# Attention rounds: scores three steps ahead, outputs of two blocks taken together a step later, denominators spread over three steps

## What is computed

```python
a = a_val * jax.nn.sigmoid(a_gate)
a = jax.nn.silu(layer_norm(causal_depthwise_conv(a, conv_w, conv_b), ln_g, ln_b))     # 31 taps, 512 channels
...
s = jnp.einsum('bqhd,bqkhd->bqhk', qb, k_sel) * (HEAD_DIM ** -0.5)                    # 8 heads of 64
p = jax.nn.softmax(jnp.where(valid[:, :, None, :], s, -jnp.inf), axis=-1)
o = jnp.einsum('bqhk,bqkhd->bqhd', p, v_sel)
...
return jnp.concatenate([a, o], axis=-1) @ w_out
```

## Time and profile before

| | us |
|---|---|
| median of three runs | 2775.15 |
| lowest and highest run | 2771.99, 2776.19 |
| span of the profiled execution | 2768.8 |
| of it, the stage `attention_and_conv` with its first loads | about 420 to 720 |
| loops 0 to 41 with their start, with taps | 434 to 595 |
| loops 42 to 71 and the end of the stage, no taps | 595 to 720.5 |

### The profile page before, as it was taken

How to read it: one execution, slowest core, us unless ns; L and a number is a source line. 1 busy time by engine, 2 the same in 40 slices (tenths; PEclk the granted TensorE clock), 3 DMA queues, 4 the chain that set the end, 5 groups by cost and what they waited for, 6 DMA issues and landing times. The chain is left out here.

```text
span 2768.8 us, 37693 instructions
## 1 busy us (share of the span) xinstructions
PE 2483.0 (90%) x12607; PEld 2105.9 (76%) x12607; DVE 2035.1 (74%) x2461; ACT 1707.5 (62%) x1832; POOL 643.2 (23%) x484
## 2 busy tenths in 40 slices
PE   8789987997895999999999589997969999999993
PEld 8779966876584888888888478986857888888882
DVE  4687775667657898888988644545468888888895
ACT  2367836655423778787777446555127777777773
POOL 0105616643001211211121212121001112222213
PEclk9899998997896999999999789999979999999996
DMA  5502233220535879998899411003347879999994
GB/s 169 124 1 93 75 95 91 83 56 6 153 107 202 330 252 365 367 375 293 293 367 361 166 66 38 32 30 110 106 161 260 320 262 371 367 366 370 374 364 145
DMA packets 115273, 565.16 MB, mean 204 GB/s; under 512 B 23520, under 2 KB 27872, under 8 KB 65904
## 3 DMA queue, kind: packets, MB, share of 16 engines
q1 hardware_dynamic: 89776, 512.15, 50.7%
q0 software_dynamic: 25408, 51.84, 6.9%
HBM read 574.22 MB, written 74.34 MB: 234 GB/s over the span
## 5 line engine op out<-in xcount | busy, mean ns | idle before, releaser
L1923 DVE TENSOR_TENSOR e0wlo<-e0raw,e0whi 128x2048 fp32r<-128x2048 f32 x214 | 486.9, 2290 | 68.6 <-ACT e0whi L1771 67.0
L1923 DVE TENSOR_TENSOR e1wlo<-e1raw,e1whi 128x2048 fp32r<-128x2048 f32 x208 | 472.9, 2289 | 66.0 <-ACT e1whi L1771 66.0
L1771 ACT ACTIVATE e0whi<-e0raw 128x2048 fp32r<-128x2048 f32 x214 | 410.0, 1916 | 103.2 <-PE e0u L90 42.1
L1771 ACT ACTIVATE e1whi<-e1raw 128x2048 fp32r<-128x2048 f32 x208 | 398.3, 1916 | 101.0 <-PE e1u L90 42.1
L88 PE MATMUL odd_ps<-h2T_hi,odd_w_hi 128*128 128x348 f32 x480 | 158.3, 330 | 6.2 <-DVE odd_w_lo L2388 6.2
L89 PE MATMUL odd_ps<-h2T_lo,odd_w_hi 128*128 128x348 f32 x480 | 155.6, 324 | 0.0
L90 PE MATMUL odd_ps<-h2T_hi,odd_w_lo 128*128 128x348 f32 x480 | 155.4, 324 | 0.0
L88 PE MATMUL m_y<-m_whi,m_xhi 128*128 128x512 f32 (+1 forms) x304 | 121.7, 400 | 22.1 <-DVE m_wlo L1503 21.6
L89 PE MATMUL m_y<-m_wlo,m_xhi 128*128 128x512 f32 (+1 forms) x304 | 119.7, 394 | 0.0
L90 PE MATMUL m_y<-m_whi,m_xlo 128*128 128x512 f32 (+1 forms) x304 | 119.7, 394 | 0.0
L88 PE MATMUL e0g<-e0whi,e0xh 128*128 128x512 f32 x284 | 115.6, 407 | 0.6 <-DVE e0xl L1928 0.6
(11 more groups left out here) (457 smaller groups left out, 7116.3 us busy)
## 6 DMA issues: line engine op xcount, KB each, us to landing
e0raw<-in_moe_w_gate SPq DMA_DIRECT2D x72, 1024.0 KB
e0raw<-in_moe_w_up SPq DMA_DIRECT2D x72, 1024.0 KB
e0raw<-in_moe_w_down SPq DMA_DIRECT2D x72, 1024.0 KB
e1raw<-in_moe_w_gate SPq DMA_DIRECT2D x70, 1024.0 KB
e1raw<-in_moe_w_up SPq DMA_DIRECT2D x70, 1024.0 KB
e1raw<-in_moe_w_down SPq DMA_DIRECT2D x70, 1024.0 KB
qki_w_raw<-in_w_even SPq DMA_DIRECT2D x22, 512.0 KB, 5.0
odd_w_raw<-in_w_odd SPq DMA_DIRECT2D x20, 512.0 KB, 3.7
```

The source lines that it names most:

```text
L1771: act.activation(w_hi[:, i, :], raw[:, i, :], ACT.Copy).then_inc(hi_done[i], 1)
L1923: dve.tensor_tensor(w_lo[:, i, :], raw[:, i, :], w_hi[:, i, :].bitcast(F32), ALU.subtract).then_inc(lo_done[i], 1)
```

## The change

- `scores` and `biased` run three steps ahead instead of two.
- `biased` writes the scaled negative row minimum of the negated scores straight to `nmx`: the scaling instruction (L1250) is gone, and exps waits for `s_read`.
- `turned`, `p_high` and `p_low` are cut into an early part (two groups) and a late one (the third group, in blocks 8 alone). On PE the late part comes after the four taps.
- On ACT, exps(n+2) stands ahead of p_high(n+1).
- The outputs of two blocks of one size (a **unit**) share a bank and are taken together, one loop after the later one's values: o_lows and take_out run once for 40 units instead of 72 times.
- Denominators are transposes, one group in each of three loops that begin two after the pair's end, and normalise follows them. The reciprocals stand ahead of p_low.
- `means` go over four loops instead of two; the branch's later parts start two loops later, the last (`OUT_AT`) one.

```diff
+AHEAD, EARLY_GROUPS, DEN_AFTER = 3, 2, 2
...
+def denominator_at(n):
+    t, g = divmod(n + 1 - DEN_AFTER - PAIR_END, PAIR_END)
+    return [(t, g)] if t >= 0 and g < 3 else []
+
+UNITS = [[n] if n % NB == 0 else [n, n + 1] for n in range(N) if n % NB == 0 or n % NB % 2 == 1]
...
-MEAN_AT, CENTRE_AT, VAR_AT, ROOT_AT, SCALE_AT, SWISH_AT, OUT_AT = (CONV_STEPS + n for n in (1, 4, 6, 11, 13, 15, 17))
+MEAN_STEPS = 4
+MEAN_AT, CENTRE_AT, VAR_AT, ROOT_AT, SCALE_AT, SWISH_AT, OUT_AT = (CONV_STEPS + n for n in (1, 6, 8, 13, 15, 17, 18))
...
+            def denominators(t, g):
+                k, js = norm_at[t][g], key_groups(NB - 1)[g]
                 pe.wait_ge(rden_done, t + 1)
-                for k, js in enumerate(key_groups(NB - 1), norm_at[t]):
-                    pe.wait_ge(t_free, k - 1)
-                    for j in js:
-                        a, q = (j % GROUP) * P, toks(j)
-                        last = pe.matmul(t_ps[k % 2][:, a:a + q],
...
+                pe.wait_ge(t_free, k - 1)
+                for j in js:
+                    a, q = (j % GROUP) * P, toks(j)
+                    last = pe.transpose(t_ps[k % 2][:, a:a + q], rden_rows[0:q, j, :, :].rearrange("p a d -> p (a d)"),
...
-            for n in range(N):
+            for n in range(N + 3 * DEN_AFTER):
                 m = FIRST_TAPS + n * (TAPS_A + TAPS_B)
-                if n + 2 < N:
-                    scores(n + 2)
+                if n + AHEAD < N:
+                    scores(n + AHEAD)
                 taps(range(min(m, TAPS), min(m + TAPS_A, TAPS)))
                 if n + 1 < N:
-                    turned(n + 1)
+                    turned(n + 1, True)
                 taps(range(min(m + TAPS_A, TAPS), min(m + TAPS_A + TAPS_B, TAPS)))
-                values(n)
-                if n % PAIR_END == PAIR_END - 1:
-                    denominators(n // PAIR_END)
...
+                if n + 1 < N:
+                    turned(n + 1, False)
+                if n < N:
+                    values(n)
+                for t, g in denominator_at(n):
+                    denominators(t, g)
...
             def exps(n):
...
-                act.wait_ge(mx_done, n + 1)
+                act.wait_ge(s_read, n + 1)
...
-            for n in range(N):
-                if n + 1 < N:
-                    p_high(n + 1)
+            for n in range(N + 1):
                 if n + 2 < N:
                     exps(n + 2)
-                o_lows(n)
+                if n + 1 < N:
+                    p_high(n + 1, True)
+                if n and UNITS[UNIT_OF[n - 1]][-1] == n - 1:
+                    o_lows(UNIT_OF[n - 1])
+                if n + 1 < N:
+                    p_high(n + 1, False)
                 beside(n)
...
-                dve.tensor_tensor_reduce(sm[0:q, n % 2, 0:w], s_ps[0:q, 0:w], score[0:q, AT[b]:AT[b] + w], 1.0,
-                                         -3.0e38, ALU.add, ALU.max, mx[0:q, i]).then_inc(s_read, 1)
-                dve.wait_ge(s_read, n + 1)
-                dve.tensor_scalar(nmx[0:q, i], mx[0:q, i], -HD ** -0.5, None, ALU.mult).then_inc(mx_done, 1)
+                dve.tensor_tensor_reduce(sm[0:q, n % 2, 0:w], s_ps[0:q, 0:w], score[0:q, AT[b]:AT[b] + w], -HD ** -0.5,
+                                         3.0e38, ALU.add, ALU.min, nmx[0:q, n % 2:n % 2 + 1]).then_inc(s_read, 1)
...
+            for n in range(N + 3 * DEN_AFTER):
+                if n + AHEAD < N:
+                    biased(n + AHEAD)
+                if n < N and n % PAIR_END == PAIR_END - 1:
+                    reciprocals(n // PAIR_END)
                 if n + 1 < N:
-                    p_low(n + 1)
...
+                    p_low(n + 1, True)
+                    p_low(n + 1, False)
+                if 0 < n <= N and UNITS[UNIT_OF[n - 1]][-1] == n - 1:
+                    take_out(UNIT_OF[n - 1])
+                for t, g in denominator_at(n):
+                    normalise(t, g)
```

More of the change, by code:

```diff
@@ L947, in attention_and_conv @@
         pT = d.sb("pT", [P, 2, NB, 2, P], F32R)
-        o_low = d.sb("o_low", [P, 2, P])
-        mx, nmx = (d.sb(n, [P, 2]) for n in ("mx", "nmx"))
+        o_low = d.sb("o_low", [P, 2, 2, P])
+        nmx = d.sb("nmx", [P, 2])
         den, rden = (d.sb(n, [P, NB, HEADS]) for n in ("den", "rden"))
@@ L971, in tile, with outputs, place, rows_of @@
             return glu4[:, W4 * t:W4 * (t + 1), 0:NPH]
+        def outputs(u):
+            return o_ps[u % 2][:].rearrange("p (i a q) -> p i a q", i=2, a=2)
+        def place(n):
+            u = UNITS[UNIT_OF[n]]
+            return 0 if len(u) == 1 else int(STEPS[n][1] == max(STEPS[m][1] for m in u))
+        def rows_of(u):
+            blocks = sorted(STEPS[n][1] for n in UNITS[u])
+            return len(blocks), toks(blocks[0]), blocks
+        def groups(n, early):
+            part = slice(0, EARLY_GROUPS) if early else slice(EARLY_GROUPS, None)
+            return list(enumerate(key_groups(STEPS[n][1]), at[n]))[part]
         def every(row):
@@ L1208, in p_high, with o_lows @@
                     act.activation(pT[0:rows, n % 2, js[0]:js[-1] + 1, 0, 0:q], src, ACT.Copy).then_inc(p_hi_done, 1)
-            def o_lows(n):
-                h, b = STEPS[n]
+            def o_lows(u):
+                h, (m, q, _) = STEPS[UNITS[u][0]][0], rows_of(u)
                 own, other = ((slice(0, HD), slice(HD, P)), (slice(HD, P), slice(0, HD)))[h % 2]
-                act.wait_ge(pv_mm, n + 1)
-                if n >= 2:
-                    act.wait_ge(o_done, n - 1)
-                act.activation(o_low[own, n % 2, 0:toks(b)], o_ps[n % 2][other, 0:toks(b)], ACT.Copy).then_inc(low_done, 1)
+                act.wait_ge(pv_mm, UNITS[u][-1] + 1)
+                if u >= 2:
+                    act.wait_ge(o_done, u - 1)
+                act.activation(o_low[own, u % 2, 0:m, 0:q], outputs(u)[other, 0:m, 0, 0:q], ACT.Copy).then_inc(low_done, 1)
             highs(0)
@@ new lines, in reciprocals, with normalise @@
+            def reciprocals(t):
+                dve.wait_ge(exp_done, PAIR_END * (t + 1))
+                dve.reciprocal(rden[:, :, 2 * t:2 * t + 2], den[:, :, 2 * t:2 * t + 2]).then_inc(rden_one, 1)
+                dve.wait_ge(rden_one, t + 1)
+                pair = rden[:, :, 2 * t:2 * t + 2].rearrange("p b (a d) -> p b a d", d=1)
+                dve.tensor_copy(rden_rows[:], pair.broadcast_to([P, NB, 2, HD])).then_inc(rden_done, 1)
+            def normalise(t, g):
+                k, js = norm_at[t][g], key_groups(NB - 1)[g]
+                dve.wait_ge(o_done, PAIR_UNITS * (t + 1))
+                dve.wait_ge(t_mm, k + 1)
+                for j0, j1 in (((0, 1), (1, GROUP)) if js[0] == 0 else ((js[0], js[-1] + 1),)):
+                    a, w = tok0(j0), tok0(j1 - 1) + toks(j1 - 1) - tok0(j0)
+                    p0 = (j0 % GROUP) * P
+                    last = dve.tensor_tensor(oT[:, t, a:a + w], t_ps[k % 2][:, p0:p0 + w], oT[:, t, a:a + w], ALU.mult)
+                last.then_inc(t_free, 1)
```

133 lines of the change are left out of this document (59 added, 74 removed).

## The result

The changed kernel takes **2739.81 us**, median of 4 runs (2735.38 to 2741.52), against 2775.67 us for the kernel before, run beside it. The ratio is 0.9869, with a 95% interval of 0.9852 to 0.9885: 36 us, or 1.3%, faster. Forecast were 2748 us and a range of 2736 to 2766.

A forecast was written before the change was run, and what follows sets the result against it. The prediction took PE as the bound up to the last tap and the order of waits behind it. Gains of 11 and 16 us from 2768.8 us gave 2741.8, plus 6.4 to the median: 2748 us, range 2736 to 2766.

The forecast's parts named there:

- First stretch: The 161.0 us up to where the taps end, 42 loops, PE the bound: 11 us gained (4 to 16).
- (1) The tap bank: Between tap groups, PE's 6.2 us of waits for ACT to take the bank mostly go: 4 us (0 to 6).
- (2) The third group: In blocks 8, four taps cover 0.6 of a 1.1 us wait: 3 us (2 to 5), less 0.5 for switches.
- (3) Two pair ends: Denominators at two pair ends in the tap stretch, 3.6 us each, partly coming back: 4 us gained (3 to 6).
- (4) The start: At the stage's start three scores go out ahead of the first exp: 0.5 us gained (0 to 2).
- Second stretch: The 125.5 us behind the taps, 30 loops and the end, no engine full: 109.5 us needed, 16 gained (5 to 22).
- PE's excess in eight loops: Behind the taps, loops with means or variances need more of PE than of DVE: 10 us on top of DVE's sum.
- The ring: Behind the taps, transposes, copies, exp and their waits stand in line, about 2.8 us a step.
- DVE's wait for the denominators: Behind the taps, an added wait for six groups that PE makes only behind values: 6 x 0.3 us.
- The ring comes back elsewhere: Rival, 0.13: copies wait behind an exp that isn't ready, then p_low, bank and PE; gain 10 us, 2765 us.
- The clock falls: Rival, 0.05: whole second stretch at 1.2 GHz, about 153 us there, 2792 us in all.
- The way through DRAM sets the end: Rival, 0.05: rows' 19 us trip after the last swish, hidden by 4 us; otherwise up to 3 lost, 2751 us.

The follow-up runs named there:

- u_early3: Changed kernel with all three groups of transposes ahead of the second set of taps; 2744.69 us, ratio 0.9888 to the kernel before.
- u_den_matmul: Changed kernel with the denominators as plain float32 matmuls again, still one group in each of three loops; 2744.34 us, ratio 0.9900 to the kernel before.
- b_ahead3: Kernel before with only scores and biased scores three steps ahead, ScalarE's order as it was; 2766.67 us, ratio 0.9968.
- b_act_ahead3: Kernel before with scores and biased scores three steps ahead and exps ahead of the copies of p on ScalarE; 2767.37 us, ratio 0.9974.
- u_ahead2: Changed kernel with scores and biased two steps ahead again, ScalarE's new order kept; 2781.76 us, ratio 1.0028 to the kernel before.
- u_single: Changed kernel with the outputs of each block taken alone, still a loop after its values; 2742.64 us, ratio 0.9888 to the kernel before.
- u_act_order: Changed kernel with exps(n+2) behind the copies and o_lows again on ScalarE; 2744.03 us, ratio 0.9890 to the kernel before.
- u_out_now: Changed kernel with outputs taken in the loop of the block, or of a pair's second block, as before; 2743.24 us, ratio 0.9881 to the kernel before.
- u_ring_back: Changed kernel with scores and biased two steps ahead and ScalarE's old order, both undone; 2745.45 us, ratio 0.9892 to the kernel before.

## Why the prediction held, and where its steps failed

**The base.** The prediction took 27 us from the profiled span and added 6.4 us to reach the median, so its forecast is the median before less 27 us. The stage gave 33.7 us: of the 8.3 us by which the forecast was too high, 6.7 are terms of the stage that were too small, 1.8 in the first stretch and 4.9 in the second. The medians differ by 2 us more than the two profiled stages, which is less than single executions differ. The forecast of the span, 2741.8 us, came within 2.6 us of the 2739.2 measured by luck: of the 6.4 us only 1.8 lie around every span, and the other 4.6 are what this execution of the kernel before lay under its median, while the profiled execution after lies 1.2 us above its own.

**First stretch, 11 us forecast, 12.8 measured.** The sum is near, its terms are not. I measured them from tap to tap, since the same tap opens the same loop in both kernels. (1) The tap bank, 4 forecast of 6.2: 5.5 us of it went. Undoing the order costs 4.7 us, undoing the outputs' place 5.3, each more than the waits for the bank that it brings back. I had named both edits as its cause, rightly, but not that neither helps without the other. (2) The third group, 3 less 0.5 for the switches of kind: 2.0 by u_early3. The wait that is left:

```profile
505.05 0.28 PE L1094 MATMUL c_ps<-g_hi,band_lo 128*128 128x260 f32 x1
...
506.33 0.30 PE L1133 MATMUL t_ps<-const,pr 128*128 128x128 f32 x1 [0.99 <-DVE pT L1297]
```

It was 1.10 us. This one, the longest, stands right behind a pair's end; in the other three of the window it is 0.71 us. So the taps cover 0.4 us of it, where the prediction had 0.6.

(3) Two pair ends, 4 forecast. The prediction took both at the 3.6 us that it had read from the first. By the taps the loop with the first pair's end is 3.2 us longer than the same loop of another head (7.08 against 3.85), that with the second 2.0 (5.89). In the changed kernel the loops with denominators and products are 1.7 and 1.4 us longer. That is 2.1 us gained, and the kind alone is worth 2.6 (u_den_matmul): nothing is left for the later place and the spread. (4) The start, 0.5 forecast. From the first tap to the one that opens loop 9 it is 46.6 us before and 45.3 after, 1.3 us gained, where the nine loops of a head without a pair's end gain 2.6 to 2.9 (32.5 before, 29.7 after). So the start lost 1.3 to 1.5 us. Up to the tap that opens loop 0 it is 13.5 us before and 14.8 after, with three scores in it instead of two.

The ordinary steps are thus worth some 12 us, where the first two terms had 6.5. In nine of them PE's wait for the bank went from 1.78 us to nothing, that for `p_low` from 1.11 to 0.71, and PE's busy time from 29.3 to 28.8 us; between 4 and 5 us in all stand in no term and no run assigns them. The stretch came out within 2 us because the ordinary steps were sized too low and both pair ends and start too high. That is luck, although the waits named are the ones that went.

**Second stretch, 16 us forecast, 20.9 measured, and here the mechanism was only half right.** I had put DVE at 89 us of need, PE's excess in eight loops at 10 us on top, and had said of the spread means that they add nothing and take nothing away except the pile-up. The norm's places are worth 7.1 us, more than any other single edit that I undid here but the distance: up to 3.3 us is the pile-up, which I named but did not price, and by the rows 3.7 us the tanh's wait for a product of the same loop, which I didn't see, though the trace of the kernel before had it twice. The change moved the product by one loop and the swish by two, and I had read both as a delay. The ring that the prediction saw in the earlier trace rows is real, but to open it alone (b_ahead3, b_act_ahead3) is worth 9 to 10 us of B, and with the rest of the change in place to close it again costs 2.4 us. The two figures for one edit say how the terms overlap, and that the gain of B is no sum of its edits: measured one by one they are 7.1 (norm), 2.4 to 10.4 (distance and order), up to 3 (spread of the denominators), and no gain in B for the late outputs (B is 3.1 us shorter without them), the pairing, the kind of the denominators and the late third group (1.6 us shorter without it). Behind the last tap no taps stand between the groups, and the third group waits 1.20, 1.20 and 0.78 us there, where the prediction had 3 x 0.5.

Single terms of that sum: the two additions of a pair of blocks take 0.43 us in the trace (0.41 forecast; means of 367 and 372 ns with the small form among them). DVE's wait for the denominators was put at 2 us in this stretch and is 2.9, of 6.2 in both; of the first stretch's two pairs it had no such term. Most of the 2.9 us stands in one place, the loop with the square root:

```profile
631.50 1.28 ACT L1214 ACT_TABLE_LOAD   x1 [0.34 <-DVE conv_spare L1335]
...
632.80 0.42 ACT L1214 ACTIVATE conv_spare<-conv_spare 128x260 f32<-128x260 f32 x1
...
633.23 1.28 ACT L1232 ACT_TABLE_LOAD   x1
...
633.59 1.12 PE L1154 MATMUL t_ps<-const,rden_rows 16*128 16x16 f32 x4
...
634.53 0.52 ACT L1232 ACTIVATE pr<-sm,nmx 128x272 f32<-128x272 f32 x1
...
634.82 0.64 DVE L1325 TENSOR_TENSOR oT<-t_ps,oT 128x16 f32<-128x16 f32 x2 [2.30 <-PE t_ps L1154]
```

The first denominators of the third pair fall in the very loop in which ACT loads its tables twice, and the granted clock is at its lower level from 630.7 to 637.5. The Trainium skill (ScalarE: Activation LUTs, What ACT_TABLE_LOAD costs) gives 1283 ns for the load, which the rows show, and some 1380 ns for a drain with each, 2.66 us a switch. The rows don't show that part here: from the first load to the exp behind the second are 3.03 us, with the square root's 0.42 in it, 1.3 us a switch. The forecast's 2 us for this loop were in the right place.

**The signs named.** First stretch of 150 us: 148.2, between the same points. Denominators as 36 rows of some 0.2 us: 36 rows of 0.325 us in the mean. No idle time of PE above 1 us ahead of the denominators: false once, 1.55 us at the last pair, where nothing is left to put in between. DVE over 75% busy in the second stretch: 79.25 of 104.60 us, 76%. The exp waits gone: yes. The clock from 640 on at 0.9 or more: no, it fell in the last 37 us.

```profile
640.00:653.00 13.00, 10.11 (x56) 7.52 (x55) 12.47 (x24) 9.41 (x21) 4.23 (x6) 0.93 0.00 1
653.00:690.00 37.00, 29.62 (x140) 22.51 (x138) 28.79 (x58) 21.51 (x52) 10.14 (x11) 0.73 0.42 116
```

**The rivals.** *The ring comes back elsewhere* was ruled out by the 0.9 us that the exp still waits, and u_ahead2 shows what it would have been: not a loss of 17 us of the gain, as I had it, but of the whole gain and 7 us more (2781.76 against 2774.59). *The clock falls*: it was low for 28.7 us of B instead of 47.8. Only u_ahead2, with its stalls, has more than the kernel before (65.4). With plain matmuls for the denominators B has 16.7 us at the low clock, with transposes 28.7; but u_single, u_early3 and u_act_order, with the same transposes, have 18.2, 18.3 and 14.8. The Trainium skill's rule that the full clock doesn't engage for transposes (TensorE: Matmul & The Clock Gate, Part 4: PE-mode transpose) isn't borne out: the first stretch of the changed kernel, with transposes in each step, has a granted clock of 0.99. How much of B's gain is the clock's is **open**: between the changed kernel and u_den_matmul 12 us more at the low clock cost 0.8 us, but in u_ahead2 and before the low clock comes with long waits, and no run separates the two.

*The way through DRAM sets the end.* It was near. SP's queue in the changed kernel, and its last rows' landing (min, median, max from issue):

```profile
666.83 5.28 SPq L1025 DMA_DIRECT2D conv_rows<-glu  x4
...
679.18 1.76 SPq L1029 DMA_DIRECT2D glu<-conv_rows  x4
...
690.19 11.11 SPq L1491 DMA_DIRECT2D m_raw<-in_w_out  x8
```

```profile
DMA to landing us min/median/max: 3.8/5.1/7.3
```

The last of the four is issued at 680.5 and lands 7.3 us later, at 687.8; the last product ends at 689.02. The cover is 1.2 us where I had 4: the way took 21.0 us from its first issue, for the 19 allowed, and the steps beside it 22.2 for 23. In u_out_now the rows come back at 691.6 (684.05 and 7.5 us), after the last product at 691.04:

```profile
682.72 1.76 SPq L1029 DMA_DIRECT2D glu<-conv_rows  x4
...
689.20 1.84 DVE L1325 TENSOR_TENSOR oT<-t_ps,oT 128x16 f32<-128x16 f32 x4
...
692.70 1.28 SPq L1491 DMA_DIRECT2D m_raw<-in_w_out  x3
```

There it sets the end, if by half a microsecond. So an edit that shortens only what lies behind the last swish can show little more than the 1.2 us of cover. A kernel that is faster than the changed one by more than a measurement can tell doesn't follow from the runs: early outputs behind the last tap alone would be the one candidate (B 3.1 us shorter in u_out_now), 0.1%; it wasn't run.

## What to carry to other kernels

Undo an edit in the finished kernel as well as adding it to the old one: here the distance is worth 7 us of the stage in the old one (9 in B, less what A loses) and 2 in the new one (u_act_order against u_ring_back), and the new order on ScalarE is worth 4 us with the distance and costs 31 without it. A resource that is freed late by a busy in-order engine (here the tap bank) needs every instruction ahead of it in that queue to be on time; here opening one lock of two moved nothing. And where no engine is full, look at the side work first: how much of it falls in one loop, and whether a buffer of its own comes free in the loop that wants it; here the norm's places gave 7 us behind the last tap, nearly as much as the opened ring alone in the old kernel.

## What the runs showed that I had not expected

- With two piles of 16 matmuls of 3.68 us each the head is 3.3 us longer than with four piles of 8 (1.92 us each), though the work is the same (part of it may be the low clock, see above). With one score buffer, biased waits for the scores behind the pile: 2.43 and 4.83 us with two piles, 3.06 and 2.52 with four.
- The start of the stage moved by up to 3.8 us (424.8 to 428.6) between executions of kernels that are the same up to there, and so did the places of the later low-clock stretches. A difference of 3 us between two profiled spans says nothing; the same difference between the same steps within the stage does.
- A plain fp32 matmul of 128 columns appears as two rows and takes 1.2 us more for nine than nine transposes do, 0.13 us each. In A this is the whole cost of the form.
